# Two layer norms and the products behind them, worked by pairs of token blocks in half-width items

## The chip, the cores and the metric

The kernel runs on one core of a Trainium2 chip. A core has TensorE (matmuls and transposes, results in the eight PSUM banks), VectorE, ScalarE and GpSimd (called DVE, ACT and POOL in the profile), and SyncE (SP), which only starts transfers here. They run their own instruction streams and wait for each other by semaphores. The metric is the time of one execution on the device, in microseconds (us), lower is better.

## The reference

The input is `x`, one sequence of 512 tokens by 1024 features in float32. The first block computes a conditioning vector from `c`, a hybrid mixer (a state-space scan and a forgetting attention), and a feed-forward; the second block a banded attention with a short convolution and a pooling, and another feed-forward. Cut to what matters here:

```
# first block
x = layer_norm(ALPHA * x + (1 + g1) * y, ln1_g, ln1_b)        # y: the mixer's output product
h = x * (1 + sc2) + sh2
ff = square(relu(h @ w_ff_in)) @ w_ff_out                     # 1024 -> 4096 -> 1024
x = layer_norm(ALPHA * x + (1 + g2) * ff, ln2_g, ln2_b)
# second block
h = rms_norm(x, norm1_g)
p = h @ w_in                                                  # q, k, v first: 3 x 512 columns
```

with `layer_norm(x) = (x - mean) / sqrt(var + eps) * g + b` over the 1024 features of a token.

## The kernel before

**Tiles.** The 512 tokens are four blocks `t` of 128. The 1024 features are eight tiles `k` of 128. `x1[:, t]` holds block `t`, tokens on the partitions. A product needs its activations turned, features on the partitions: `a_hi[0][:, k]` and `a_lo[0][:, k]`, each 128 x 512 tokens. Each product is done as three matmuls (`three`, lines 1700 to 1704), high by high, high by low and low by high, because a value is held as a rounded part and a rest.

**Weights.** They come in units of 128 x 2048 through two slots, unit `u` in slot `u % 2`. A unit is loaded into `raw` (SyncE), rounded into `w_hi` (ScalarE, `hi`, line 740, once `ticks` says that the slot's unit before has been used), and its rest `w_lo` is made by four subtractions of 512 columns (GpSimd, `lo`, line 546). TensorE waits for `w_lo_made`, which counts whole units. A unit feeds 48 matmuls of 512 columns. In the feed-forward a unit of `w_ff_in` (`columns`) gives two output tiles of 128 hidden features by 512 tokens, with the weights stationary; in `row_pair` two units give an output of four token blocks by 512 columns, with the activations stationary and weights moving.

**Order.** Every engine's order is written out by hand. At the first norm: VectorE reads the last product's banks, adds (line 1580), and takes statistics per block (`half_stats`, lines 1208 to 1212); GpSimd makes the root (`ln_root`, line 539); VectorE makes the shift (line 1217); ScalarE normalises blocks 0 to 2 whole (`normalize`, line 753), VectorE block 3 (`normalize_last`, line 1225). TensorE turns the blocks (`turn_blocks`, line 1777), 32 transposes, into banks 0 to 7, one bank per feature tile with all four blocks. Then ScalarE makes the high part of each tile (line 748) and its negated rest (line 761), 512 columns each, and VectorE the low part (`split_affine`, line 1161). Between block 2 and the tiles ScalarE rounds the second unit. VectorE then applies gain and bias to `x1` (`gain`, lines 1232 and 1233). The first two output tiles follow the feature tiles as they come (`two_tiles`), the other products behind them.

The second norm, at the end of the first feed-forward, is made in the same way (sum on line 1599) and feeds `row_pair(U_QKV2, ...)`, whose two units give the first 512 of the columns. Then ScalarE sums squares for the RMS norm (`squares`, line 779), reads the product's banks (`read_rows`, line 773), and GpSimd makes the head roots (line 525).

In the feed-forward ScalarE reads a finished tile (line 838), squares it (line 840), and rounds the next but one unit behind the first two tiles of a pair; VectorE makes the hidden tile's low part (lines 1249 and 1149).

## Time and profile before

| | |
|---|---|
| median of 3 runs | 1438.65 us (1436.66 to 1438.85) |
| profiled execution | 1433.96 us, its span 1432.2 us |
| mean granted TensorE clock in it | 0.994 |
| TensorE matmul busy | 1370.6 us, 96% |
| VectorE, ScalarE, GpSimd busy | 698.0, 547.4, 688.3 us |

The span runs from the first to the last instruction of the profiled execution; 1.8 us of its time lie around it. Ends of matmuls are modelled: neighbours overlap in the list, so the distance from start to start is what one costs. The granted clock is a share of full speed.

### The profile page before, as it was taken

Reading aid. Unit: us, or ns where it says so; the run is one execution under the profiler, and the core shown is the slowest. Engines: PE = TensorE matmul, PEld = TensorE weight load, DVE = VectorE, ACT = ScalarE, POOL = GpSimd, SP = SyncE. Lnnn points to the kernel's source line nnn. Section 1 sums busy time; section 2 is a strip of 40 time slices with the busy share of each in tenths; the row PEclk is TensorE's granted clock in tenths of the full one; section 3 lists DMA queues with packets and bytes.
Section 4 is the critical chain, followed back from the end, with each engine's and each line's share of the span. In section 5 each row is a group of like instructions: output and inputs, shape, how many; then the busy total and the mean of one; then the engine's idle time right before and its main releaser. Section 6 shows DMA issues by size and latency. Waiting matters only on the chain.

```text
span 1432.2 us, 17281 instructions
## 1 busy us (share of the span) xinstructions
PE 1370.6 (96%) x6567; PEld 1124.0 (78%) x6567; DVE 698.0 (49%) x1005; ACT 547.4 (38%) x793; POOL 688.3 (48%) x544
## 2 busy tenths in 40 slices
PE   2999999999999999999999998999999999999999
PEld 2887787778777878888888886886788888888887
DVE  6676978788843672141324456357623213132231
ACT  0635454476662262141332316324525223132231
POOL 0453855332346655445445544753644445445442
PEclk9999999999999999999999999999999999999999
DMA  9353445755323432322232232342122332232232
GB/s 331 116 136 93 98 129 173 207 142 150 104 59 130 146 92 88 109 96 88 88 117 88 88 110 72 105 120 77 45 93 89 105 101 88 92 102 99 88 98 78
DMA packets 132249, 158.58 MB, mean 111 GB/s; under 512 B 9469, under 2 KB 93713, under 8 KB 131937
## 3 DMA queue, kind: packets, MB, share of 16 engines
q1 hardware_dynamic: 123760, 146.95, 32.6%
q10 hardware_dynamic: 6240, 5.40, 1.7%
q0 software_dynamic: 2192, 5.49, 1.2%
q8 instruction: 34, 0.56, 0.2%
q14 instruction: 23, 0.18, 0.0%
HBM read 153.47 MB, written 2.26 MB: 109 GB/s over the span
## 4 chain that ended last, share of the span: by engine, by line
PE 81%; DVE 9%; POOL 3%; issue 2%; ACT 2%; DMA 1%; SPq 0%; ACTq 0%; DVEq 0%; POOLq 0%
PE bank L1702 25%; PE bank L1703 24%; PE bank L1704 24%; DVE tmp L1268 3%; POOL w_lo L546 3%; PE bank L1839 1%; DMA arena<-in_w_ada_dram 1%; DVE rinv L1175 1%; PE bank L1970 1%; PE bank L2208 1%; PE bank L1824 1%; ACT w_hi L740 1%; PE bank L1849 1%; PE bank L2026 1%; PE bank L1852 1%
## 5 line engine op out<-in xcount | busy, mean ns | idle before, releaser
L546 POOL TENSOR_TENSOR w_lo<-raw,w_hi 128x512 fp32r<-128x512 f32 x428 | 585.2, 1399 | 605.9 <-ACT w_hi L740 604.7
L1702 PE MATMUL bank<-w_hi,a_hi 128*128 128x512 f32 x928 | 365.3, 394 | 13.3 <-POOL w_lo L546 6.5
L1703 PE MATMUL bank<-w_lo,a_hi 128*128 128x512 f32 x928 | 362.6, 391 | 0.0
L1704 PE MATMUL bank<-w_hi,a_lo 128*128 128x512 f32 x928 | 362.6, 391 | 0.0
L740 ACT ACTIVATE w_hi<-raw 128x2048 fp32r<-128x2048 f32 x107 | 204.7, 1913 | 356.8 <-PE bank L1704 353.6
L1702 PE MATMUL bank<-a_hi,w_hi 128*128 128x512 f32 x800 | 315.7, 395 | 3.4 <-DVE a_lo L1161 2.5
L1703 PE MATMUL bank<-a_lo,w_hi 128*128 128x512 f32 x800 | 312.2, 390 | 0.0
L1704 PE MATMUL bank<-a_hi,w_lo 128*128 128x512 f32 x800 | 312.0, 390 | 0.0
L1702 PEld LDWEIGHTS bank<-w_hi,a_hi 128*128 128x128 f32 x928 | 175.1, 189 | 51.7 <-DVE a_lo L1161 6.2
L1704 PEld LDWEIGHTS bank<-w_hi,a_lo 128*128 128x128 f32 x928 | 175.0, 189 | 36.9
L1703 PEld LDWEIGHTS bank<-w_lo,a_hi 128*128 128x128 f32 x928 | 175.1, 189 | 35.7
L1702 PEld LDWEIGHTS bank<-a_hi,w_hi 128*128 128x128 f32 x800 | 150.7, 188 | 35.4 <-issue 2.7
L1704 PEld LDWEIGHTS bank<-a_hi,w_lo 128*128 128x128 f32 x800 | 150.7, 188 | 31.9
L1703 PEld LDWEIGHTS bank<-a_lo,w_hi 128*128 128x128 f32 x800 | 150.9, 189 | 30.6 <-issue 0.2
L1249 DVE TENSOR_TENSOR tmp<-arena 128x512 f32<-128x512 f32 x64 | 64.6, 1009 | 189.3 <-ACT arena L838 189.3
L838 ACT ACTIVATE arena<-bank 128x512 f32<-128x512 f32 x64 | 38.4, 599 | 210.9 <-PE bank L1704 203.3
L1691 DVE SCALAR_TENSOR_TENSOR arena<-bank,st,arena 128x512 f32<-128x512 f32 x32 | 24.0, 751 | 144.6 <-PE bank L1704 144.6
L1268 DVE SCALAR_TENSOR_TENSOR tmp<-arena,cact,tmp 128x256 f32<-128x256 f32 (+1 forms) x140 | 88.2, 630 | 4.9 <-DMA arena<-in_w_ada_dram 0.3
L1149 DVE TENSOR_TENSOR a_lo<-tmp,a_hi 128x512 fp32r<-128x512 f32 x64 | 66.7, 1043 | 7.2
L1591 DVE TENSOR_TENSOR arena<-bank,arena 128x512 f32<-128x512 f32 x24 | 16.6, 692 | 109.6 <-PE bank L1704 109.6
L787 ACT ACTIVATE arena<-bank,mxs 128x128 f32<-128x128 f32 (+1 forms) x96 | 49.5, 533 | 35.7 <-DVE mxs L1179 35.5
L825 ACT ACTIVATE arena<-bank 128x512 f32<-128x512 f32 (+1 forms) x72 | 33.2, 526 | 22.2 <-PE bank L1839 17.5
(248 smaller groups left out, 1258.6 us busy)
## 6 DMA issues: line engine op xcount, KB each, us to landing
raw<-in_w_mlp_dram SPq DMA_DIRECT2D x32, 1024.0 KB, 5.3
raw<-in_w_in_dram SPq DMA_DIRECT2D x24, 1024.0 KB, 5.2
arena<-in_w_ada_dram SPq DMA_DIRECT2D x18, 1024.0 KB, 6.5
raw<-in_w_ff_in_dram SPq DMA_DIRECT2D x16, 1024.0 KB, 5.4
raw<-in_w_ff_out_dram SPq DMA_DIRECT2D x16, 1024.0 KB, 5.1
raw<-in_w_out_dram SPq DMA_DIRECT2D x12, 1024.0 KB, 5.6
raw<-in_w_in_dram SPq DMA_DIRECT2D x16, 512.0 KB, 5.7
arena<-in_w_ada_dram SPq DMA_DIRECT2D x3, 2048.0 KB, 18.1
```

The source lines that it names most:

```text
L546: last = pool.tensor_tensor(w_lo[:, u0 % 2, cols], raw[:, u0 % 2, cols], w_hi[:, u0 % 2, cols].bitcast(F32), ALU.subtract)
L740: act.activation(w_hi[:, u0 % 2], raw[:, u0 % 2], ACT.Copy).then_inc(w_hi_made, 1)
L787: act.activation(dst[:, QO[q]:QO[q] + n], src(q), ACT.Exp, bias=mxs[:, h % 2, q:q + 1], accum_out=rsum[:, h % 2, q:q + 1]).then_inc(p_made, 1)
L825: act.activation(dst[:, 512 * m:512 * m + n * P], bank[b][:, 0:n * P], ACT.Copy).then_inc(pt_made, 1)
L838: act.activation(rl[:, k % 2], bank[4 * b + j][:], ACT.Relu).then_inc(evac[b], 1)
L1149: dve.tensor_tensor(a_lo[buf][:, k], tmp[:, m0 % 2], a_hi[buf][:, k].bitcast(F32), ALU.subtract)\
L1249: dve.tensor_tensor(tmp[:, k % 2], rl[:, k % 2], rl[:, k % 2], ALU.mult).then_inc(tile_made, 1)
L1268: ins = dve.scalar_tensor_tensor(acc, src(k), cact[:, k:k + 1], acc, ALU.mult, ALU.add)
L1691: dve.scalar_tensor_tensor(x1[:, t, part], bank[4 * b + t][:], st[:, 12 + t:13 + t], x1[:, t, part], ALU.mult, ALU.add).then_inc(evac[b], 1)
L1702: pe.matmul(out_, hi_a, hi_b, start=start, stop=False)
L1703: pe.matmul(out_, hi_a, lo_b, start=False, stop=False)
L1704: return pe.matmul(out_, lo_a, hi_b, start=False, stop=stop)
```

## The change

- An item is a pair of token blocks (256 columns) of one feature tile. `LN_ITEMS` lists 16: features 0 to 3 of blocks 0 and 1, of blocks 2 and 3, then features 4 to 7 in the same order. Transposes go to halves of banks 4 to 7.
- ScalarE normalises blocks 0 and 1, VectorE blocks 2 and 3 in halves, and the statistics of block 3's second half, the four half normalisations and the low parts of the items are interleaved in `last_tokens`. The shift of block 0 comes one block earlier.
- TensorE starts with the first eight transposes and puts the other 24 behind items 1, 3 and 7.
- At the first norm the first four output tiles (`first_columns`) are made in passes: features 0 to 3 with the first unit, then with the second, then features 4 to 7 with the first and the second, in matmuls of 256 columns, 192 in place of 96. The first quarter of the feed-forward is taken out of TensorE's loop.
- At the second norm `first_rows` goes item by item, for two token blocks each, in matmuls of 512 columns.
- The second unit at either norm is rounded on GpSimd in quarters, each followed by its subtraction (`both_parts`), with a semaphore `lo_part` for the first three.
- ScalarE rounds the third unit at the second norm ahead of items 12 to 15, the fourth ahead of the first reads, and the sixth between two pairs of reads. GpSimd makes the row loads ahead of the quarters and the mask behind them.

```diff
+LN_ITEMS = [(pair, 4 * half + k) for half in range(2) for pair in range(2) for k in range(4)]
...
+        def turned_item(pair, k):
+            return bank[4 + 2 * pair + k % 2][:, 256 * (k % 4 // 2):256 * (k % 4 // 2) + 256]
...
+            def both_parts(u0):
+                pool.wait_ge(landed[u0 % 2], 16 * (u0 // 2 + u0 % 2 + pairs_loaded(u0)))
+                pool.wait_ge(ticks, 2 * u0 - 2)
+                for part in range(4):
+                    cols = slice(512 * part, 512 * part + 512)
+                    ins = pool.tensor_copy(w_hi[:, u0 % 2, cols], raw[:, u0 % 2, cols])
+                    if part == 0:
+                        ins.then_inc(w_hi_made, 1)
+                        pool.wait_ge(w_hi_made, u0 + 1)
+                    else:
+                        link(ins)
+                    ins = pool.tensor_tensor(w_lo[:, u0 % 2, cols], raw[:, u0 % 2, cols], w_hi[:, u0 % 2, cols].bitcast(F32), ALU.subtract)
+                    ins.then_inc(lo_part if part < 3 else w_lo_made, 1)
...
-            ln_root(0)
-            pool.wait_ge(xhat_last, 2)
-            lo(U_FF1 + 1)
+            lo(U_WO2 + 4, turn=0)
+            for t in range(1, TB):
+                ln_root(0, t)
+            both_parts(U_FF1 + 1)
...
+            def affine_items(r0, t0, scale, bias, js):
+                def rest(j):
+                    pair, k = LN_ITEMS[j]
+                    act.wait_ge(a_hi_made, t0 + j + 1)
+                    act.wait_ge(a_lo_made, t0 + max(j - 3, 0))
+                    act.activation(rest_item(j), a_hi[0][:, k, tokens(pair)].bitcast(F32), ACT.Identity, scale=-1.0, bias=bias(k)).then_inc(tile_made, 1)
+                for j in js:
+                    pair, k = LN_ITEMS[j]
+                    act.wait_ge(turned, r0 + j // 4 * 4 + 3 + j % 2)
+                    if j % 4 >= 2:
+                        act.wait_ge(a_lo_made, t0 + j - 1)
+                    act.activation(a_hi[0][:, k, tokens(pair)], turned_item(pair, k), ACT.Identity, scale=scale(k), bias=bias(k)).then_inc(a_hi_made, 1)
+                    rest(j)
...
-            for t in range(TB - 1):
+            for t in range(2):
                 normalize(1, t)
-            hi(U_QKV2 + 1)
-            turned_affine(R_N2, T_N2, 0, ...)
+            for js in (range(12), range(12, 16)):
+                affine_items(R_N2, T_N2, ..., js)
+                if js[0] == 0:
+                    act.wait_ge(w_hi_made, U_QKV2 + 2)
+                    hi(U_QKV2 + 2)
-            hi(U_QKV2 + 2)
             squares(2, x1, junk, ln_made, lambda t: 4 + t + 1)
+            hi(U_QKV2 + 3)
...
+            def last_tokens(turn, m0, scale):
+                split_item(0, m0, scale)
+                half_stats(TB - 1, 1)
+                split_item(1, m0, scale)
+                normalize_half(turn, 2, 0)
+                normalize_half(turn, 3, 0)
+                split_item(2, m0, scale)
+                split_item(3, m0, scale)
+                normalize_half(turn, 2, 1)
+                normalize_half(turn, 3, 1)
+                for j in range(4, 16):
+                    split_item(j, m0, scale)
...
+            def first_columns():
+                first_turned(0, N_FF1)
+                for half in range(2):
+                    for n0 in (0, 2):
+                        u = U_FF1 + n0 // 2
+                        if half == 0 and n0 == 0:
+                            pe.wait_ge(w_lo_made, u + 1)
+                        for j in range(8 * half, 8 * half + 8):
+                            pair, k = LN_ITEMS[j]
+                            if n0 == 0:
+                                pe.wait_ge(a_lo_made, T_X1 + j + 1)
+                            elif pair == 0 and k % 2 == 0:
+                                wait_part(u, 0, k // 2)
+                            for n in (n0, n0 + 1):
+                                w = slice(256 * k + P * (n % 2), 256 * k + P * (n % 2) + P)
+                                last = three(bank[n][:, tokens(pair)], w_hi[:, u % 2, w], w_lo[:, u % 2, w],
+                                             a_hi[0][:, k, tokens(pair)], a_lo[0][:, k, tokens(pair)], j == 0, j == 15)
+                                if j == 15:
+                                    last.then_inc(ticks, 1)
+                            if n0 == 0:
+                                turn_behind(0, T_X1, N_FF1, j)
+
+            def first_rows():
+                first_turned(1, N_QKV2)
+                for j, (pair, k) in enumerate(LN_ITEMS):
+                    u = U_QKV2 + k // 4
...
+                    pe.wait_ge(a_lo_made, T_N2 + j + 1)
+                    for t in (2 * pair, 2 * pair + 1):
+                        a, w = slice(P * t, P * t + P), slice(512 * (k % 4), 512 * (k % 4) + 512)
+                        last = three(bank[t][:], a_hi[0][:, k, a], a_lo[0][:, k, a], w_hi[:, u % 2, w], w_lo[:, u % 2, w],
+                                     k == 0, k == KT - 1)
...
+                    turn_behind(1, T_N2, N_QKV2, j)
```

## Rows read from the trace of the kernel before

**Rows 1.** The page, busy time of TensorE: us, share of the span, instructions.
```profile
PE 1370.6 (96%) x6567; PEld 1124.0 (78%) x6567; DVE 698.0 (49%) x1005; ACT 547.4 (38%) x793; POOL 688.3 (48%) x544
```

**Rows 2.** Timeline of TensorE, first norm: start, us, operation, idle before, releaser.
```profile
499.83 0.39 PE L1704 MATMUL bank<-w_hi,a_lo 128*128 128x512 f32 x1
...
505.00 1.11 PE L1777 MATMUL bank<-ident,arena 128*128 128x128 f32 x8 [0.60 <-DVE arena L1225]
508.36 0.47 PE L1702 MATMUL bank<-a_hi,w_hi 128*128 128x512 f32 x1 [2.24 <-DVE a_lo L1161]
...
532.35 0.39 PE L1702 MATMUL bank<-a_hi,w_hi 128*128 128x512 f32 x1
```

**Rows 3.** Timeline of TensorE, second norm.
```profile
858.52 0.39 PE L1704 MATMUL bank<-w_hi,a_lo 128*128 128x512 f32 x1
...
870.75 0.80 PE L1702 MATMUL bank<-w_hi,a_hi 128*128 128x512 f32 x1 [5.99 <-DVE a_lo L1161]
...
894.56 0.39 PE L1702 MATMUL bank<-w_hi,a_hi 128*128 128x512 f32 x1
```

**Rows 4.** Stretches, TensorE: from, to, us, busy, granted clock, DMA share, GB/s.
```profile
510.00:511.00 1.00, 1.00 (x4) 0.50 0.00 0
```

**Rows 5.** Timeline of TensorE, two other waits for weights.
```profile
248.32 0.50 PE L1702 MATMUL bank<-w_hi,a_hi 128*128 128x512 f32 x1 [2.30 <-POOL w_lo L546]
...
454.84 0.61 PE L1702 MATMUL bank<-w_hi,a_hi 128*128 128x512 f32 x1 [1.85 <-POOL w_lo L546]
```

**Rows 6.** Timelines of VectorE and ScalarE, first norm: sums and normalisations.
```profile
496.37 1.09 DVE L1580 TENSOR_TENSOR arena<-arena 128x512 f32<-128x512 f32 x1
...
501.90 0.68 DVE L1580 TENSOR_TENSOR arena<-arena 128x512 f32<-128x512 f32 x1
...
499.38 2.37 ACT L753 ACTIVATE arena<-arena,st 128x1024 f32<-128x1024 f32 x2 [8.03 <-DVE st L1217]
```

**Rows 7.** Groups of ScalarE by line and shape: busy us, mean ns, idle before.
```profile
L748 ACT ACTIVATE a_hi<-bank,mod 128x512 fp32r<-128x512 f32 x24 | 18.5, 780 | 0.7 <-PE bank L1777 0.6
L761 ACT ACTIVATE tmp<-a_hi,mod 128x512 f32<-128x512 f32 x24 | 17.1, 728 | 0.0
...
L825 ACT ACTIVATE arena<-bank 128x512 f32<-128x512 f32 x48 | 26.2, 595 | 19.0 <-PE bank L1839 14.4 <-DMA inv_d<-rinv 4.3
...
L825 ACT ACTIVATE arena<-bank 128x256 f32<-128x256 f32 x24 | 9.3, 389 | 3.2 <-PE bank L1839 3.1
```

**Rows 8.** Timeline of TensorE, score matmuls of 256 columns, and the next.
```profile
368.92 0.33 PE L2026 MATMUL bank<-k_split,q_split 128*128 128x256 f32 x1
369.10 0.28 PE L2027 MATMUL bank<-k_split,q_split 128*128 128x256 f32 x1
369.21 0.34 PE L2026 MATMUL bank<-k_split,q_split 128*128 128x384 f32 x1
```

**Rows 9.** Timelines of ScalarE and GpSimd: the feed-forward's third unit.
```profile
520.39 0.60 ACT L838 ACTIVATE arena<-bank 128x512 f32<-128x512 f32 x1 [4.67 <-PE bank L1704]
...
522.92 1.90 ACT L740 ACTIVATE w_hi<-raw 128x2048 fp32r<-128x2048 f32 x1
...
524.90 6.90 POOL L546 TENSOR_TENSOR w_lo<-raw,w_hi 128x512 fp32r<-128x512 f32 x4 [9.21 <-ACT w_hi L740]
```

**Rows 10.** Groups of GpSimd by line and shape: casts of 512 elements.
```profile
L579 POOL CAST q_split<-ones 64x512 fp32r<-64x512 f32 x4 | 5.0, 1258 | 0.4 <-POOL w_lo L546 0.2
...
L554 POOL CAST arena<-arena 16x512 fp32r<-16x512 f32 x1 | 0.6, 607 | 0.1
```

**Rows 11.** Behind the second norm: timeline of VectorE, ScalarE's group of squares, GpSimd's timeline.
```profile
878.51 1.23 DVE L1232 TENSOR_TENSOR arena<-arena 128x1024 f32<-128x1024 f32 x1 [3.31 <-DMA arena<-in_ln_b_dram]
...
L779 ACT ACTIVATE arena<-arena 128x1024 f32<-128x1024 f32 x12 | 12.7, 1060 | 0.3
...
898.61 5.42 POOL L546 TENSOR_TENSOR w_lo<-raw,w_hi 128x512 fp32r<-128x512 f32 x4 [4.39 <-ACT w_hi L740]
```

**Rows 12.** Timeline of TensorE, first product of the stage behind the second norm's.
```profile
940.22 0.47 PE L1702 MATMUL bank<-a_hi,w_hi 128*128 128x512 f32 x1 [0.88 <-POOL w_lo L546]
```

179 lines of the change are left out of this document (105 added, 74 removed).

## The prediction

> **What bounds the kernel now.** I read the profile page's busy times first [rows 1]: TensorE is busy for 96% of the span, so a change counts only where TensorE waits, runs at the lower clock, or gets more instructions. Then I read its timeline where the diff acts. At the first norm the last output product starts at 499.83, the last transposes run at 505.00, the first product behind them waits another 2.24 and starts at 508.36, and the third weight unit starts at 532.35 [rows 2]. At the second the same steps stand 358.69 later, but the first product waits 5.99 for the fourth low tile and starts at 870.75; the third unit starts at 894.56 [rows 3]. Two units are 96 matmuls, at 0.2267 each (between starts of neighbours at full clock) 21.8 us. They took 24.0 and 23.8: the difference of 2 us is mostly clock, granted at 0.50 (the 1.2 GHz level) behind the first wait [rows 4]; the 0.80 of the matmul at 870.75 shows the same behind the second. Shorter waits can do it too: 1.85 us ahead of 454.84 was followed by matmuls of 0.61, while 2.30 ahead of 248.32 was not (0.50) [rows 5]. From 532.35 to 858.52 are 326.17, and the 1439 matmuls started between need 326.2: TensorE has no slack there, and a wait put there adds itself whole.
>
> So about 8.5 us lie between last product and first product at the first norm, 12.2 at the second. Not all is to be had: 32 transposes stay. Eight take 1.11 with their drain [rows 2], that is 0.12 each, 3.9 for 32.
>
> **First norm: an earlier start.** VectorE's shift of block 0 moves right behind the sum of block 1, which ends at 497.46 [rows 6], and the root on GpSimd moves ahead of the last quarter of the unit before. ScalarE's two normalisations (1.2 each) can then end near 500.75 instead of 501.75 [rows 6]; statistics and root of block 1 stand between them. Eight transposes later ScalarE starts on item 0 at about 501.45. An item is two activations of 256 columns. At 512 columns they take 0.78 and 0.73; going from 512 to 256 columns took 0.21 off a copy from PSUM (0.595 to 0.389) [rows 7]. So 0.57 and 0.52; the second waits for the end of the first, with hand-overs 1.12 a pair. VectorE is free at 502.6, when the sum of block 3 ends [rows 6], and needs 0.5 for its part: first product at 503.2, 5.2 earlier than now. But 16 items of 1.12 are 17.9 on ScalarE, against 8 pairs of at most 1.51 now, and item 7 is ready only at 511.1.
>
> **First norm: the products.** Each item lets TensorE do 6 matmuls of 256 columns. No product of this kernel has that shape; the nearest are score matmuls of 256 columns with the same weight load, of which one started 0.11 after the other [rows 8]. The bounds are 0.11 and, from half of 213 plus the 14 ns that stand over 512 columns' 213, 0.12; if a pair like the one behind 368.92 (0.18 to the next) were the rule, 0.18. I take 0.12: 0.72 per item, less than 1.12, so TensorE follows ScalarE through the first half and ends item 7 at 511.9. Behind it come 8 transposes (1.0), pass 2 of the first half (48 matmuls, 5.8) and pass 1 of the second half (5.8): 524.4, and 0.5 for a low clock while it works in drips, so 524.9. Pass 2 ends it at 530.7. That alone would be 1.7 earlier than 532.35.
>
> The Trainium skill, TensorE: Matmul & The Clock Gate, Back-to-back issue gap, gives N/2.4 + 2.5 ns between matmuls at full clock, 109 ns for 256 columns and 216 for 512. The rows have 227 for 512, so I stay with the rows; by the page's figure the 96 matmuls ahead of 524.9 that nothing hides would take 1.0 less, and the sum below would be 1.9 instead of 2.9.
>
> **First norm: what is late next.** Now the first unit is given back after its own 48 matmuls, at about 521.4, and the second is used for 10.9 more. In the new order both units stay in use to the last half pass: the first unit's slot is free at 524.9, and only 5.8 of work are left. The way to the third unit's weights is in the rows [rows 9]: ScalarE starts its reads at 520.39, two reads and two squares (2.53) stand ahead of the rounding at 522.92, which takes 1.90, and GpSimd's four subtractions take 6.90, to 531.80; today that is 0.55 ahead of need. The same chain from 524.9 is 2.5 + 1.9 + 0.1 + 6.9 + 0.1: 536.4. VectorE's gain pass now ends near 530 and its hidden tiles follow, so the subtractions run beside it as they do now; with less beside them they take 5.4 [rows 11]. TensorE stands still for 5.7. The wait is as long as that of [rows 3], so I add its clock loss, 1.9. First norm: 536.4 - 532.35 + 1.9 = 6.0 **lost**; bounds 2 (subtractions at 5.4, clock kept throughout) and 8.5 (the low clock all through the first half too).
>
> **The quarters on GpSimd.** A quarter copy of 128x512 is not in the trace. Nearest are casts of 0.6 and 1.26 for 512 elements [rows 10]; with a subtraction of 1.3 to 1.7 a quarter takes 2 to 3. Block 3's statistics and root end at 504.8; from there part 0 is ready by 507.9 and part 3 by 517; needed from 512.9 on. At the second norm all is 358.7 later behind two row loads, and the need comes at 876.6. Both stay hidden behind the first half, and would cost only if two quarters took over 8. Taking the rounding (1.90) off ScalarE is what lets item 0 follow the transposes at once; that gain is in the starts above.
>
> **Second norm.** Here weights are the moving side: matmuls stay at 512 columns and their number stays. First product at 503.2 + 358.7 = 861.9; an item now carries 6 x 0.2267 = 1.36 us of work, more than ScalarE's 1.12, so TensorE is the pace. 21.8 of matmuls, 24 transposes among them (3.0), 0.1 of waits, 0.7 for the clock: second unit ends at 887.5, 7.1 earlier than 894.56. The third unit is ready: its slot is free behind item 7 (861.9 + 8 x 1.36 + 2.0 of transposes + 0.8: 875.7), ScalarE rounds it behind item 11, GpSimd ends by 884.6. The fourth is not. ScalarE does items 12 to 15 only after that rounding: 875.7 + 2.0 + 4.5 + 0.6 = 882.8 for the last low tile. Then VectorE's gain pass, 8 operations of 1.23 [rows 11] and a little for its start beside the subtractions, to 892.9; the last square with its sum 1.25, the fourth unit's rounding 1.9, behind the squares in ScalarE's queue, subtractions 5.4 [rows 11]: ready at 901.7. Needed at 887.5 + 10.9 = 898.4. A wait of 3.3, and 1.5 for the clock, between nothing [rows 5] and the 2.0 of [rows 3]. Today the fourth starts at 894.56 + 10.9 = 905.4. So 3.7 gained at its start, 2.2 once the clock is paid.
>
> Further on, today TensorE waits 0.88 at 940.22 for the weights of the next stage, behind two head roots on GpSimd [rows 12]. The sixth unit's rounding moves ahead of the second pair of reads (1.3), which starts that row of GpSimd work 1.3 sooner, so 0.9 goes. Second norm: 2.2 + 0.9 = 3.1 **gained**; bounds 1 (a full clock loss at both places) and 6 (none).
>
> Other moved steps (row loads, ahead of the quarters; the mask, behind them) issue as many DMAs as before and are wanted 10 us later. The unrolled first quarter adds no work.
>
> **Sum.** 6.0 - 3.1 = 2.9 lost. The profiled execution took 1433.96 (span 1432.2 and 1.8 around it); with the change 1436.9. The median of the runs is 4.7 above it, so 1438.65 + 2.9 = 1441.6, just over the 0.2% (2.9 us) that a measurement of this kernel can tell from no change.
>
> **Rivals.**
> - *Clock kept* (ends on the other side): no low clock behind the new waits, as ahead of 248.32 [rows 5]. Takes off 1.9 + 1.5 + 0.5 + 0.7 = 4.6: 1437.0, no change. Any saving over 0.1 decides. Against it: the wait of 5.7. Chance 0.13.
> - *Subtractions undisturbed*: 5.4 instead of 6.9 for the third unit takes off 1.5: 1440.1, no change. Against it, [rows 9]. 0.19.
> - *Third unit in time*: TensorE reaches it at 530.7 and goes on. 1.7 + 3.1 gained: 1433.8, faster. It decides, with the clock then kept, if the chain behind 524.9 takes under 7.6, where I count 11.5; for it speaks only that the chain's rounding and reads might overlap. 0.12.
> - *Half-size matmuls at 0.18*: 96 x 0.06 = 5.8 more: 1447.4, slower. Speaks for it one pair of starts. 0.09.
> - My forecast: 0.47, of which 0.07 falls within 0.2%.
>
> Slower 0.40 + 0.09 = 0.49, within 0.2% 0.13 + 0.19 + 0.07 = 0.39, faster 0.12. The range leaves out the third and fourth rival: 1436 to 1446.5, with the forecast's own case from 1439.5 to 1444.
>
> **What would show it.** Right: first products 5 us earlier at the first norm, 9 at the second; starts of 256-column matmuls 0.12 apart; one wait of 4 to 6 us for GpSimd's low part ahead of the third unit of the feed-forward, matmuls of 0.63 behind it; a wait of about 3 ahead of the fourth unit at the second norm. Wrong: no wait ahead of the third unit, or subtractions well under 6.9 there, or the gain pass starting before the last low tile.

## The result, and the profile after

The changed kernel takes 1448.74 us (median of 4 runs, 1448.13 to 1448.97), the kernel before in the same session 1437.66 (4 runs): ratio 1.0078, 95% interval 1.0061 to 1.0095. Timed again with the experiments it was 1.0070 (1.0043 to 1.0096). It is slower; 1441.6 was predicted.

The page's line of busy times, after:

```profile
PE 1382.3 (96%) x6663; PEld 1138.1 (79%) x6663; DVE 704.2 (49%) x1023; ACT 552.1 (38%) x821; POOL 694.2 (48%) x552
```

TensorE has its 96 matmuls more and is as full as before [rows 1]; the span grew from 1432.2 to 1446.9. The timeline of TensorE around the first norm:

```profile
504.39 0.39 PE L1773 MATMUL bank<-w_hi,a_lo 128*128 128x512 f32 x1
...
508.50 0.55 PE L1771 MATMUL bank<-a_hi,w_hi 128*128 128x256 f32 x1 [1.83 <-DVE a_lo L1218]
...
535.71 0.28 PE L1772 MATMUL bank<-a_lo,w_hi 128*128 128x256 f32 x1
535.83 0.28 PE L1773 MATMUL bank<-a_hi,w_lo 128*128 128x256 f32 x1
541.40 0.77 PE L1771 MATMUL bank<-a_hi,w_hi 128*128 128x512 f32 x1 [5.28 <-POOL w_lo L576]
...
545.38 0.48 PE L1771 MATMUL bank<-a_hi,w_hi 128*128 128x512 f32 x1
```

Counted from the start of the last product before the norm, the first product comes after 4.11 us (8.53 before [rows 2]), the half passes end 31.6 us after it, and then TensorE waits 5.28 for the third unit, which starts after 37.01, not 32.52 as before. Nine matmuls at the half clock (granted 0.50; 0.427 apart) follow. The timelines of ScalarE and GpSimd say what it waited for:

```profile
532.44 1.90 ACT L771 ACTIVATE w_hi<-raw 128x2048 fp32r<-128x2048 f32 x1
...
534.42 6.83 POOL L576 TENSOR_TENSOR w_lo<-raw,w_hi 128x512 fp32r<-128x512 f32 x4 [11.01 <-ACT w_hi L771]
```

It is the chain of [rows 9], whose subtractions now begin 30.0 us after the last product and not 25.1. The timeline of TensorE behind the second norm:

```profile
869.65 0.39 PE L1773 MATMUL bank<-w_hi,a_lo 128*128 128x512 f32 x1
...
873.70 0.76 PE L1771 MATMUL bank<-w_hi,a_hi 128*128 128x512 f32 x1 [1.79 <-DVE a_lo L1218]
...
915.12 0.79 PE L1771 MATMUL bank<-w_hi,a_hi 128*128 128x512 f32 x1 [4.41 <-POOL w_lo L576]
...
920.83 0.49 PE L1772 MATMUL bank<-w_lo,a_hi 128*128 128x512 f32 x1
...
953.20 0.47 PE L1771 MATMUL bank<-a_hi,w_hi 128*128 128x512 f32 x1 [1.48 <-POOL w_lo L576]
```

The first product comes 4.05 us after the last one instead of 12.23 [rows 3], but the fourth unit is waited for 4.41 and started after 45.47; thirteen matmuls at the half clock follow, and the wait for U_CP (the seventh unit, the first of the next stage) grew from 0.88 [rows 12] to 1.48. The first product of that stage stands 83.55 us after the last one before the norm, 1.85 later than before (81.70). What the fourth unit and U_CP's wait for, in the timelines of VectorE, ScalarE and GpSimd:

```profile
894.11 0.48 DVE L1218 SCALAR_TENSOR_TENSOR a_lo<-bank,mod,tmp 128x256 fp32r<-128x256 f32 x1 [0.51 <-ACT tmp L806]
894.51 1.79 DVE L1301 TENSOR_TENSOR arena<-arena 128x1024 f32<-128x1024 f32 x1
...
904.84 1.06 ACT L826 ACTIVATE arena<-arena 128x1024 f32<-128x1024 f32 x1 [1.24 <-DVE arena L1302]
...
906.02 1.92 ACT L771 ACTIVATE w_hi<-raw 128x2048 fp32r<-128x2048 f32 x1
...
908.02 11.98 POOL L576 TENSOR_TENSOR w_lo<-raw,w_hi 128x512 fp32r<-128x512 f32 x8 [0.62 <-ACT w_hi L771]
...
931.16 7.14 POOL L576 TENSOR_TENSOR w_lo<-raw,w_hi 128x512 fp32r<-128x512 f32 x4 [5.33 <-ACT w_hi L771]
938.38 2.15 POOL L538 TENSOR_SCALAR st<-head_rs 128x32 f32<-128x32 f32 x1
```

Last low tile, gain pass, four squares, rounding, subtractions: one chain. The fourth unit's subtractions end as TensorE starts, at 915.1, so they took 7.1 us (the row of eight is two units).

**Where 14.7 us of span went.** By the last products before the norms, the spans differ by 4.56 ahead of the first, 6.57 from the first to the second (365.26 against 358.69), and 3.57 from there to the end. The first of the three lies in code that the change doesn't touch. The stretches of TensorE (from, to, us, busy, granted clock, DMA share, GB/s) show it; these are the kernel before in its first profile, then in a second one, then the changed kernel:

```profile
180.00:200.00 20.00, 18.82 (x97) 1.00 0.29 96
240.00:260.00 20.00, 17.70 (x84) 1.00 0.86 252
1035.00:1060.00 25.00, 22.84 (x110) 1.00 0.28 90
```
```profile
180.00:200.00 20.00, 18.82 (x81) 0.83 0.31 104
240.00:260.00 20.00, 17.70 (x78) 0.91 0.88 260
1035.00:1060.00 25.00, 22.84 (x123) 1.00 0.24 73
```
```profile
180.00:200.00 20.00, 18.82 (x82) 0.83 0.31 99
240.00:260.00 20.00, 17.70 (x78) 0.91 0.89 257
1035.00:1060.00 25.00, 22.84 (x129) 0.93 0.30 96
```

The kernel before loses the same clock in some executions: against its second profile (span 1436.9, last products at 504.06 and 862.97) the change costs 10.0. Of the 3.57 behind the second norm, 1.7 is clock at 1035 to 1060 (0.07 of 25 us), far from the change; the kernel before has full clock there in both profiles.

### The profile page after: what moved, and what is told of

It reads as the page before. It is cut to its first block, busy times and chain, and to the rows that moved or that the text cites. A ratio compares the mean times of both kernels' runs of the same rounds, so it can differ in the third digit from the quotient of the medians.

```text
span 1446.9 us, 17550 instructions
## 1 busy us (share of the span) xinstructions
PE 1382.3 (96%) x6663; PEld 1138.1 (79%) x6663; DVE 704.2 (49%) x1023; ACT 552.1 (38%) x821; POOL 694.2 (48%) x552
## 4 chain that ended last, share of the span: by engine, by line
PE 78%; DVE 10%; POOL 5%; issue 3%; ACT 2%; DMA 1%; SPq 0%; ACTq 0%; POOLq 0%; DVEq 0%
PE bank L1771 24%; PE bank L1773 23%; PE bank L1772 23%; POOL w_lo L576 4%; DVE tmp L1337 3%; PE bank L1968 1%; DMA arena<-in_w_ada_dram 1%; ACT w_hi L771 1%; PE bank L2099 1%; PE bank L2337 1%; PE bank L1953 1%; DVE rinv L1232 1%; PE bank L1978 1%; PE bank L2155 1%; PE bank L1981 1%
## 5 line engine op out<-in xcount | busy, mean ns | idle before, releaser
L576 POOL TENSOR_TENSOR w_lo<-raw,w_hi 128x512 fp32r<-128x512 f32 x420 | 574.6, 1399 | 602.5 <-ACT w_hi L771 602.5
L1771 PE MATMUL bank<-w_hi,a_hi 128*128 128x512 f32 x928 | 367.9, 396 | 13.5 <-POOL w_lo L576 10.9
L771 ACT ACTIVATE w_hi<-raw 128x2048 fp32r<-128x2048 f32 x105 | 200.9, 1913 | 346.9 <-PE bank L1773 342.8
L1771 PE MATMUL bank<-a_hi,w_hi 128*128 128x512 f32 (+1 forms) x832 | 323.1, 388 | 8.6 <-POOL w_lo L576 6.8
L1772 PE MATMUL bank<-a_lo,w_hi 128*128 128x512 f32 (+1 forms) x832 | 319.0, 383 | 0.0
L1773 PE MATMUL bank<-a_hi,w_lo 128*128 128x512 f32 (+1 forms) x832 | 318.9, 383 | 0.0
L1771 PEld LDWEIGHTS bank<-a_hi,w_hi 128*128 128x128 f32 x832 | 157.9, 190 | 39.7 <-issue 9.4
L1773 PEld LDWEIGHTS bank<-a_hi,w_lo 128*128 128x128 f32 x832 | 157.8, 190 | 30.5
L1772 PEld LDWEIGHTS bank<-a_lo,w_hi 128*128 128x128 f32 x832 | 158.1, 190 | 29.7 <-issue 0.2
L1250 DVE TENSOR_TENSOR arena<-bank,arena 64x256 f32<-64x256 f32 x48 | 29.5, 614 | 25.2 <-PE bank L1981 24.6
```

Of the source, the lines that this page charges most:

```text
L576: last = pool.tensor_tensor(w_lo[:, u0 % 2, cols], raw[:, u0 % 2, cols], w_hi[:, u0 % 2, cols].bitcast(F32), ALU.subtract)
L771: act.activation(w_hi[:, u0 % 2], raw[:, u0 % 2], ACT.Copy).then_inc(w_hi_made, 1)
L1250: last = dve.tensor_tensor(by_query(att_pair(h)[own(h % 2)], side), value_out(side), inverse_rows(h, side), ALU.mult)
L1771: pe.matmul(out_, hi_a, hi_b, start=start, stop=False)
L1772: pe.matmul(out_, hi_a, lo_b, start=False, stop=False)
L1773: return pe.matmul(out_, lo_a, hi_b, start=False, stop=stop)
```

## The experiments

Two stages are compared for each kernel, both from TensorE's timeline: A, from the last product before the first norm to the last before the second; B, from there to the end of the span. Both leave out the early clock, but not the half clock inside them. So how well a stage repeats was read from kernels that have the same code in it. Stage A with the first norm of before was profiled six times: 357.59 to 359.32. With the changed one it took 364.65 to 365.65 (three), with the changed one by quarters 358.61 to 359.66 (three). Stage B with the second norm of before took 573.68 and 573.93, with the changed one as it is 572.69 to 577.26 (seven). A difference of 1 to 2 us between two single profiles therefore tells little. B is split at U_CP's first product as well: from there to the end are 491.95 to 492.05 us in eight profiles and 493.46 to 493.70 in the other eight, whatever the waits ahead; the two groups differ in how long the half clock was granted there.

Medians and ratios are of whole times, which hold the early clock too. The kernel before had medians of 1437.64, 1434.34, 1437.90 and 1436.90 in the four sessions of the experiments; its times lie in two groups, so the recorded ratio need not be the quotient of the medians (third by quarters: 0.9999, while the medians give 1.0023).

| kernel | last products | A | B | of B, up to U_CP | median us | ratio, 95% |
|---|---|---|---|---|---|---|
| before | 499.83, 858.52 | 358.69 | 573.68 | 81.70 | | |
| before again | 504.06, 862.97 | 358.91 | 573.93 | 81.94 | | |
| changed | 504.39, 869.65 | 365.26 | 577.25 | 83.55 | 1448.74 | 1.0078 (1.0061 to 1.0095) |
| changed again | 503.99, 869.64 | 365.65 | 577.26 | 83.62 | 1446.02 | 1.0070 (1.0043 to 1.0096) |
| fourth early | 500.05, 864.70 | 364.65 | 571.00 | 77.47 | 1437.99 | 1.0018 (0.9999 to 1.0036) |
| third by quarters | 505.64, 864.25 | 358.61 | 572.85 | 80.81 | 1437.61 | 0.9999 (0.998 to 1.0018) |
| rounding first | 499.21, 864.04 | 364.83 | 574.46 | 82.41 | 1440.18 | 1.0047 (1.0027 to 1.0066) |
| first unit whole | 504.34, 866.69 | 362.35 | 573.01 | 81.02 | 1440.26 | 1.003 (1.0013 to 1.0048) |
| kept busy | 499.49, 863.55 | 364.06 | 574.45 | 82.50 | 1440.61 | 1.0043 (1.0026 to 1.0061) |
| rounded on ScalarE | 500.96, 868.28 | 367.32 | 578.22 | 84.74 | 1451.67 | 1.0099 (1.0062 to 1.0137) |
| second norm as it is, alone | 499.28, 858.21 | 358.93 | 572.69 | 80.71 | 1437.87 | 1.0011 (0.9989 to 1.0032) |
| second norm alone, fourth early | 510.77, 869.66 | 358.89 | 569.64 | 76.02 | 1434.45 | 0.9983 (0.9967 to 1.0) |
| both repairs | 498.61, 857.89 | 359.28 | 569.71 | 76.02 | 1433.63 | 0.9978 (0.9959 to 0.9996) |
| both, roots later | 504.21, 863.87 | 359.66 | 567.13 | 73.65 | 1429.76 | 0.9943 (0.9922 to 0.9964) |
| second alone, fourth early, roots later | 503.62, 861.21 | 357.59 | 568.69 | 75.23 | 1431.78 | 0.9956 (0.9937 to 0.9975) |
| before, root later | 504.51, 863.83 | 359.32 | 573.57 | 81.55 | 1434.46 | 0.9984 (0.9969 to 0.9999) |

**The kernel before, once more.** No edit.

> The kernel before, unchanged, profiled once more. In the two profiles at hand everything before the first norm stands 4.56 us later after the change (last product's start 504.39 against 499.83), in code that the change does not touch, and the stretch behind U_CP's first product is 1.7 us longer. If that is the variation of single executions (the profiled one of before was among its fast ones, 1433.96 us against a median of 1437.66), this profile stands at a span of some 1435 to 1437 us with its last product before the first norm at 501 to 504. If the changed program itself costs that time, this profile repeats 499.8 and 1432.2.

It took 1438.67 us, with the clock rows shown above. The early difference is a matter of execution, not of the change. These two profiles agree to 0.2 us in A and 0.3 in B; over all runs a stage repeats less well, as said above.

**The fourth unit's rounding after the first square.**

```diff
 # ScalarE
-            squares(2, x1, junk, ln_made, lambda t: 4 + t + 1)
+            squares(2, x1, junk, ln_made, lambda t: 4 + t + 1, (0,))
             hi(U_QKV2 + 3)
+            squares(2, x1, junk, ln_made, lambda t: 4 + t + 1, (1, 2, 3))
 # GpSimd
-            rms_root(2, EPS2)
             lo(U_QKV2 + 3)
+            rms_root(2, EPS2)
```

> The changed kernel with the fourth unit behind the second norm rounded after the first of the four squares on ScalarE, not after the fourth, and its subtraction on GpSimd ahead of the root. Theory (the fourth unit is late because its rounding stands behind the gain pass and the squares): the rounding starts near 899.6 us instead of 906.0, the subtraction ends near 909 instead of 915.1, the wait of 4.41 us and the clock loss of 2.85 us behind it go, 7 us in all: about 1441.5 us. Rival (the wait is set by GpSimd and by contention with VectorE, not by the order): the subtraction, now beside the gain pass, takes 9 us or more, and less than 3 us are gained: 1446 us or more.

Timelines of ScalarE, GpSimd and TensorE:

```profile
892.70 1.06 ACT L826 ACTIVATE arena<-arena 128x1024 f32<-128x1024 f32 x1 [3.52 <-DVE arena L1303]
...
895.04 1.92 ACT L771 ACTIVATE w_hi<-raw 128x2048 fp32r<-128x2048 f32 x1 [1.20 <-PE bank L1774]
...
897.04 7.29 POOL L576 TENSOR_TENSOR w_lo<-raw,w_hi 128x512 fp32r<-128x512 f32 x4 [6.72 <-ACT w_hi L771]
...
929.23 0.50 PE L1772 MATMUL bank<-w_hi,a_hi 128*128 128x512 f32 x1 [1.67 <-POOL w_lo L576]
```

The wait for the fourth unit and the half clock behind it are gone, and B is 6.25 shorter, 2.7 under before. The order was the cause of the wait: beside the gain pass the subtractions took 7.29, hardly more than 7.1, so the rival falls. What the wait cost is read up to U_CP, from runs with the late fourth unit and the same clock behind the first product: 77.47 against 82.41 and 82.50 (rounding first, kept busy), and 76.02 against 80.71 for the second norm alone, below. That is 4.7 to 5.0 us. Of B's 6.25, 1.1 is a half clock that lasted longer in the changed kernel's own profiles; and the runs with the fourth unit early give 1.5 to 1.6 back to the clock behind U_CP, so that in B 3.1 to 3.5 are left. The whole time, 1437.99, lies below the 1441.5 expected, but it holds the early clock, which this profile (last product at 500.05) did not lose and the changed kernel's did. The next late unit shows up, the sixth, with 1.67.

**The first unit over all items, then the second in whole tiles.**

```diff
-                for half in range(2):
-                    for n0 in (0, 2):
...
+                for j in range(16):            # first unit, 256 columns
...
+                    turn_behind(0, T_X1, N_FF1, j)
+                for n in range(2):             # second unit, 512 columns
+                    column_tile(U_FF1 + 1, n, 0, bank[2 + n][:])
 # ScalarE, ahead of the feed-forward
+            act.wait_ge(w_lo_made, U_FF1 + 2)
```

> The changed kernel with the first unit behind the first norm multiplied over all sixteen items in 256 columns, and the second unit after it in whole tiles of 512 columns, so that the first slot is free after the sixteenth item. Theory (the third unit is late because both first units are held to the last half pass): the first unit ends near 525 us, the second near 535.5, the third unit is rounded by 529 and ready by 536, its wait falls from 5.28 us to under 1, and the 2.1 us of clock behind it go: 6 to 7 us gained, about 1442 us. Rival (matmuls of half the width are the cost): 48 of the 96 extra matmuls go, at most 48 x 0.013 = 0.6 us more than their columns ask for; if this were the cause, the wait would stay and the time fall to 1448 us. Second rival: TensorE, which has the work of one unit alone while the items are made (0.72 us for each 1.0), stays at the half clock to the sixteenth item, and 3 us of the gain go back: 1445 us.

Timelines of ScalarE, GpSimd, VectorE and TensorE:

```profile
528.04 1.91 ACT L771 ACTIVATE w_hi<-raw 128x2048 fp32r<-128x2048 f32 x1
...
530.03 8.63 POOL L576 TENSOR_TENSOR w_lo<-raw,w_hi 128x512 fp32r<-128x512 f32 x4 [6.66 <-ACT w_hi L771]
...
529.63 1.22 DVE L1302 TENSOR_TENSOR arena<-arena 128x1024 f32<-128x1024 f32 x1
530.88 2.20 DVE L1303 TENSOR_TENSOR arena<-arena 128x1024 f32<-128x1024 f32 x1
533.00 2.31 DVE L1302 TENSOR_TENSOR arena<-arena 128x1024 f32<-128x1024 f32 x1
...
538.81 0.77 PE L1772 MATMUL bank<-a_hi,w_hi 128*128 128x512 f32 x1 [1.94 <-POOL w_lo L576]
```

The rounding came 4.35 us earlier against the last product (23.70 after it, 28.05 in the changed kernel), as the theory has it. But the subtractions, now beside VectorE's gain pass, took 8.63 instead of 6.83, and slowed that pass too: its operations take 1.22 ahead of them and 2.20 to 2.31 beside them. 1.94 of wait stayed, with a half clock behind it. A is 2.9 shorter, under half of the 6 to 7 expected. The span is 7.2 shorter, but 4.2 of that lies in B, where code and waits (4.4 and 1.5) are those of the changed kernel.

**TensorE kept busy through the wait.**

```diff
                         first_columns()
+                        for m in range(22):
+                            pe.matmul(bank[4][:], a_hi[0][:, m % 8, 0:P], a_hi[0][:, m % 8], start=True, stop=True)
```

> The changed kernel with 22 matmuls of 512 columns added behind the half passes, into a bank that the next tile starts anew, so that TensorE works through most of the wait of 5.28 us for the third unit. Theory (the half clock after that wait is a cost of its own, 2.1 us): the third unit starts no earlier than now, near 541.4 us, but the nine matmuls at the half clock behind it run at the full one: 1446.6 us. Rival (the half clock costs nothing there because GpSimd's next units are late as well): the time stays at 1448.7 us.

TensorE's timeline:

```profile
532.14 5.18 PE L2232 MATMUL bank<-a_hi 128*128 128x512 f32 x22
537.27 0.47 PE L1771 MATMUL bank<-a_hi,w_hi 128*128 128x512 f32 x1
```

The third unit starts 37.78 after the last product, no earlier than in the changed kernel, and what follows runs at full clock: from its start to the second norm's last product 326.28, as before (326.17), against 328.25. So 2.0 of A is the half clock alone; 0.8 of it was given back ahead of the start. The whole time fell to 1440.61, not to the 1446.6 expected: the profile also lacks the early half clock (last product at 499.49), and its B is 2.8 shorter with the same code and waits, so the whole time doesn't measure this edit.

**The third unit handed over by quarters.**

```diff
 # TensorE, first tile of the third unit
+                        for k in range(KT):
+                            if k % 2 == 0 and k < 6:
+                                pe.wait_ge(lo_part, 3 + k // 2 + 1)
+                            elif k == 6:
+                                pe.wait_ge(w_lo_made, u0 + 3)
+                            last = column_step(u0 + 2, 0, 0, bank[4][:], k)
 # GpSimd: each of the four subtractions signals
+                    ins.then_inc(lo_part if part < 3 else w_lo_made, 1)
```

> The changed kernel with the third unit behind the first norm handed over by quarters: GpSimd signals each of its four subtractions, and TensorE's first tile of that unit waits for a quarter at a time (the loop over the quarters of the feed-forward is written out for its first turn on GpSimd and TensorE). Theory (the wait of 5.28 us is the time that the whole unit's rounding and subtraction take, and only the first quarter of it has to be waited for): the first product of the third unit starts near 32 us after the last product before the norm, not 37.0, right behind the half passes; the four quarters end at the same time as before, so its first tile, 5.5 us long, ends near 38.5 instead of 44.7 (with the half clock): 5 to 6 us gained in this stage. Rival: TensorE stutters through the first tile (1.7 us a quarter of which it works 1.4) and the clock falls all the same: 3.5 us gained.

Timelines of GpSimd and TensorE:

```profile
534.99 6.93 POOL L574 TENSOR_TENSOR w_lo<-raw,w_hi 128x512 fp32r<-128x512 f32 x4 [10.37 <-ACT w_hi L783]
...
536.95 0.47 PE L1783 MATMUL bank<-a_hi,w_hi 128*128 128x512 f32 x1 [0.26 <-POOL w_lo L574]
...
538.56 0.50 PE L1783 MATMUL bank<-a_hi,w_hi 128*128 128x512 f32 x1
```

The subtractions are as late and as long as before, but the third unit's first product comes 31.31 after the last product, not 37.01, and each quarter arrives just as the last is used up (0.16 to 0.22 lost at the start of each). The clock stays at full through all of A, which is 358.61: 6.65 shorter and equal to before. The same code gave 359.28 and 359.66 in the two variants with both repairs, where the half clock stands behind the first product as in the changed kernel, so the quarters give back 5.0 to 7.0, 6.0 on the means. Nearly all of the first norm's loss was this wait and its clock; over three profiles against six, 0.5 is left of it, within the spread, and no gain shows.

**The third unit's rounding ahead of the reads.**

```diff
 # ScalarE, first turn of the feed-forward written out
-                        if j == 2:
+                        if early and b == 0:
+                            if j == 0:
+                                hi(u0 + 2)
+                        elif j == 2:
                             hi(u0 + 2 * b + 2, i, 8)
```

> The changed kernel with ScalarE rounding the third unit ahead of the first two reads and squares of the hidden tiles instead of behind them (its loop written out for the first turn). Theory: the rounding starts at 30.1 instead of 32.4 us of 'after' counted, 2.3 us earlier, and the subtraction and the third unit with it: the wait of 5.28 us falls to some 3.0, the half clock behind it stays: 2.3 us gained in this stage. Rival: the subtraction, now beside the gain pass on VectorE, lengthens from 6.8 to 8.6 us, as it did where the first unit was finished early, and only 0.5 us are gained.

Timelines of ScalarE, GpSimd and TensorE:

```profile
525.47 1.92 ACT L771 ACTIVATE w_hi<-raw 128x2048 fp32r<-128x2048 f32 x1 [6.06 <-PE bank L1777]
...
527.47 7.49 POOL L576 TENSOR_TENSOR w_lo<-raw,w_hi 128x512 fp32r<-128x512 f32 x4 [9.23 <-ACT w_hi L771]
...
535.10 0.77 PE L1775 MATMUL bank<-a_hi,w_hi 128*128 128x512 f32 x1 [3.97 <-POOL w_lo L576]
```

The rounding is 1.8 earlier, the subtractions 0.7 longer, the third unit 1.1 earlier (2.3 expected), A 0.4 to 0.8 shorter than in the changed kernel's two profiles. The rival is nearer: who moves these subtractions forward moves them into VectorE's gain pass.

**The changed kernel, timed again.**

> The changed kernel itself, timed again. Six profiles so far fall into two groups by the granted clock of 180 to 200 and 240 to 260 us, code that no variant touches: 1.00 in both (before, and the variants with the fourth unit early and with TensorE kept busy) or 0.83 and 0.91 (before again, the changed kernel, the variant with the first unit whole), 4.6 us apart by the last product before the first norm. The kernel before shows both: 12 of its 29 times lie from 1432.0 to 1435.4, 17 from 1437.5 to 1441.5. Theory (the four times of the changed kernel, 1448.13 to 1448.97, all had the half clock there, and the change itself costs 10 us): some of its times now lie near 1444, and the median between 1444 and 1449. Rival (the changed program always loses that clock): all lie from 1448 to 1449.

Its times were 1442.96 to 1443.52 (three, mean granted clock 0.990) and 1448.52 to 1451.59 (three, 0.985 to 0.987): the theory holds, its first four times were all of the longer sort. This profile (1448.63) is again of the longer sort and repeats stage B to 0.01 us; an execution of the shorter sort was never profiled.

**Second norm alone, fourth unit early.** First norm's code as before; second norm's as changed, with the edit above.

> The first norm as in the kernel before, the second norm by pairs of blocks as in the changed one, with the fourth unit rounded after the first square. Theory (the first norm's part is worth -5.9 to -6.6 us, the second norm's with this order +2.8): from the last product before the second norm to the end 571.0 us, as in the variant with the fourth unit early, against 573.7 and 573.9 in the two profiles of before; from the first norm's last product to the second's 358.8 as before; 2.8 us faster than before, about 1434.8 us. Rival (the new second norm pays only because the stage before it was disturbed): within 1 us of before.

A is as before, B 569.64, 4.0 to 4.3 under it, more than the 2.8 expected. The whole time, 0.9983 (0.9967 to 1.0000), shows less of it than the stages do, which leave the early clock out. This kernel's profile lost more of it than any other (last product at 510.77), and its 12 times lie from 1429.23 to 1441.07; the early stretches of TensorE:

```profile
240.00:260.00 20.00, 17.70 (x70) 0.83 0.89 258
280.00:300.00 20.00, 17.80 (x95) 0.83 0.57 159
```

**Both repairs.** The two edits above together.

> The changed kernel with both repairs: the third unit behind the first norm handed over by quarters, and the fourth unit behind the second norm rounded after the first square. Theory (the two late units are the whole of the loss): from the first norm's last product to the second's 358.6 us, as with the quarters alone, and from there to the end 571.0 us, as with the fourth unit early alone: 2.7 to 3 us less than before in the same stages (358.7 + 573.7), a time about 0.2% under before. Rival (the clock gives back what the waits lose: the two gains do not add): equal to before within 1 us.

The gains add: A 359.28, B 569.71, and the time is 0.22% under before.

**Both repairs, and the head roots one unit later.**

```diff
             lo(U_QKV2 + 4)
-            head_root(0)
             lo(U_QKV2 + 5)
+            head_root(0)
+            lo(U_CP)
             head_root(1)
```

> Both repairs, and on GpSimd the two roots of the head norms (5.4 us each) moved one unit back, behind the subtractions of the sixth unit and of U_CP. Theory: the waits for those two units, 1.67 and 0.88 us with the fourth unit early, go, and 2.5 us are gained over the variant with both repairs, 4.2 if the half clock near 979 us (of 'start of the profile' counted) goes with them. Rival (the root that is now late holds VectorE's normalisation and TensorE's transposes of q and k): the gain is under 1 us.

TensorE's waits from 860 to 1000 us (releaser: us in total, times, longest):

```profile
PE bank L2362 <- ACT arena L847: 2.9, 1, 2.9
PE bank L1785 <- DVE a_lo L1232: 1.8, 1, 1.8
...
```

TensorE waits for no weight unit any more, and no wait of its own goes back to the later roots; B is 2.6 shorter than with both repairs (567.13 against 569.71), 2.4 of it up to U_CP. This is the best version: 0.57% under before (0.36% to 0.78%).

> First norm as in the kernel before; second norm by pairs with the fourth unit rounded after the first square; and the two roots of the head norms behind the subtractions of the sixth unit and of U_CP. Theory: 569.6 us from the second norm's last product to the end with the second norm alone; 2.5 us less with the two waits gone: 567 us, 6.5 us less than before. Rival (roots late): 569.6 stays.

The same roots without the first norm's change give 0.9956: B is 568.69, only 0.95 under the variant without the later roots, where 2.5 was expected. The same waits are gone; but a half clock stands behind the first product here (0.83 in the 10 us from the last product, 1.00 in the variant without the later roots). Against the variant that has it too (fourth early), the later roots give 2.24 up to U_CP (75.23 and 77.47), and 2.37 without it on either side (73.65 and 76.02). Both intervals of the whole time overlap widely; whether the first norm's halves are worth keeping was not told apart.

**The second units rounded on ScalarE.**

```diff
 # ScalarE, at both norms
             for t in range(2):
                 normalize(0, t)
+            hi(U_FF1 + 1)
             affine_items(...)
 # GpSimd: quarters of subtractions only
-                    ins = pool.tensor_copy(w_hi[:, u0 % 2, cols], raw[:, u0 % 2, cols])
```

> The changed kernel with the second unit behind each norm rounded by ScalarE in one instruction of 1.9 us, between the normalisations and the first item, as the kernel before did; GpSimd only subtracts, by quarters. Theory (the quarters on GpSimd are hidden and keep ScalarE free): the first items are made 1.9 us later at either norm, the stage behind the first norm takes 367 us instead of 365.3, and the one behind the second 579 instead of 577.3: 3.8 us slower than the changed kernel. Rival (GpSimd's rounding beside VectorE slows the first items and pays nothing): no slower than the changed kernel.

The first products come 5.10 and 5.08 us after the last ones, 1.0 later than in the changed kernel and not the 1.9 expected; the third unit starts at 38.67 instead of 37.01, the fourth at 47.83 instead of 45.47. A is 1.7 to 2.1 longer, B 1.0. So the quarters on GpSimd pay at these starts. The whole time, 1.0099 (1.0062 to 1.0137, four runs), is not told apart from the changed kernel's.

**Second norm as it is, alone; and a root moved in the kernel before.**

> First norm as in the kernel before, second norm exactly as in the changed kernel (fourth unit after the four squares). The stretch from the second norm's last product to the end was 577.25 and 577.26 us in two profiles of the changed kernel, but 572.85 to 574.46 us in three variants whose code from there on is the same and whose waits there are the same (4.4 and 1.5 us). Theory (those waits cost what the pairs gain, and the rest is how much of the half clock falls on work): 572.9 to 574.5 us, within 1 us of before, and a time within 0.2% of before. Rival (the second norm's part by itself costs the 3.4 us that the changed kernel shows): 577 us, and a time 0.25% above before.

B is 572.69, 1.0 to 1.2 under before, at the same waits (4.40 and 1.45) as in the changed kernel; the whole time is that of before (1.0011, 0.9989 to 1.0032). TensorE from the last product to U_CP's, first in this kernel, then in the changed one:

```profile
858.21:938.92 80.71, 72.30 (x331) 0.98 0.26 90
```
```profile
869.65:953.20 83.55, 75.09 (x330) 0.94 0.26 87
```

The same products kept TensorE busy for 72.30 us here and 75.09 there, at 0.98 and 0.94 of the clock: 2.79 of the 2.84 between the two stretches. Three stretches hold the whole difference in B, 4.56. They are the first 10 us, the fourth unit's wait with what follows, and 30 to 36 us behind U_CP's first product, in this kernel and then in the changed one:

```profile
858.21:868.21 10.00, 7.45 (x40) 1.00 0.50 187
898.21:908.21 10.00, 5.93 (x20) 0.83 0.32 105
968.72:974.72 6.00, 3.39 (x22) 1.00 0.19 65
```
```profile
869.65:879.65 10.00, 7.43 (x34) 0.83 0.51 190
911.05:921.05 10.00, 5.93 (x14) 0.66 0.34 107
983.00:989.00 6.00, 3.35 (x11) 0.74 0.23 80
```

TensorE is busy for the same time in each and does less in it. The fourth unit starts 44.07 us after the last product instead of 45.47 (1.40), six matmuls behind it run at the half clock instead of thirteen (1.44), and from U_CP's first product to the end are 491.98 instead of 493.70 (1.72). Third by quarters and first unit whole, with the late fourth unit as well and 1.00 in the first 10 us, start it at 44.09 and 44.12; rounding first and kept busy, with 0.83 there, at 45.64 and 45.65.

The second norm's part as it is gains 0.7 to 1.2 us up to U_CP where the clock stays full behind the first product (80.71 to 81.02 against 81.70 and 81.94, three profiles) and loses 0.5 to 1.9 where it doesn't (82.41 to 83.62, four). The whole time shows neither.

> The kernel before with one of the two roots of the head norms moved behind U_CP's subtraction, and nothing of the change. Theory (the gain of the moved roots in the variants comes from the waits for the sixth unit and U_CP, of which before has only the second, 0.88 us): 0.9 us faster than before, within what the measurement tells. Rival (the half clock that before has near 973 us comes from that wait and goes with it): 2.6 us faster.

Only one of the two roots is moved here. B is 573.57, 0.1 to 0.4 shorter; the wait of 0.88 is replaced by one of 0.5. The half clock near 973 us is gone, and one near 1041 stands in its place (granted 0.89 at 1035 to 1050, 1.00 in the same stretch of before). The ratio is 0.16% under 1 with an interval that ends at 0.9999. Up to U_CP it is 81.55, 0.15 to 0.4 shorter, where both later roots gave 2.2 to 2.4 with the fourth unit early. So most of that gain exists only once the waits ahead of the roots are gone, as far as one moved root can show it.

## Why the prediction was wrong

1441.6 was predicted, with 1446.5 as the upper end; 1448.7 was measured. The sign was right, and so was the first norm. The step that failed is the second norm's sum: 3.1 gained was predicted, 3.3 to 3.6 lost was measured.

- **First norm, earlier start.** 3.4 us after the last product; measured 4.11. ScalarE's items take 0.55 and 0.51 (0.57 and 0.52 predicted).
- **First norm, products.** 0.12 between starts of 256 columns, measured 0.12 (535.71 to 535.83); half passes ended 31.6 after the last product, predicted 30.9. The rival of 0.18 is out.
- **First norm, what is late next.** The step that carried the forecast: third unit ready 36.6 after the last product, wait 5.7, clock 1.9, loss 6.0. Measured 37.0, 5.28, 1.9 (541.40 to 545.38 holds nine matmuls, 3.98 less 9 x 0.2267), loss 6.57 against the first profile of before, 6.35 against the second. The subtractions took 6.83. By quarters nearly all of the loss is gone, by filling the wait the clock's part is gone: mechanism and both terms are shown, and the rivals of a third unit in time, undisturbed subtractions and a clock kept are out.
- **Quarters on GpSimd.** Hidden, as predicted; copies took 0.60 to 0.80, near the lower bound. Rounding on ScalarE instead costs 1.7 to 2.1 and 1.0 in the stages.
- **Second norm: the fourth unit.** Predicted: ready 43.2 after the last product, 3.7 gained at its start, 2.2 after the clock. The chain was right. Its term that was too small in every profile is the subtractions: **5.4 was predicted, 7.1 was measured** beside ScalarE's reads and VectorE's 2048-element pass. The gain pass ended 35.1 after the last product (34.4 predicted), but 33.7 in the second norm alone, whose first products had the full clock. Ready at 45.5, so 1.4 gained.
- **Second norm: its clock.** Behind the wait 1.5 was predicted and 2.8 lost (915.12 to 920.83 holds thirteen matmuls: 5.71 - 2.95), so -1.4 instead of +2.2. The second norm alone, with the same wait, lost 1.4 there (902.28 to 905.00 holds six): the mechanism was right, and its size differs from profile to profile.
- **Second norm: U_CP's wait.** "0.9 goes" was wrong. The sixth unit's rounding was not held by the reads it was moved past but by its slot, which the late fourth unit frees late: its subtractions start 61.5 after the last product, 61.2 before. Behind them one small multiplication, beside VectorE's normalisation of q, took 2.15 us against 0.23. The wait grew to 1.48. With the fourth unit early it is 0.88 again.
- **Second norm: clock that the sum holds at nothing.** 1.7 us more is lost behind U_CP. Against before it lies at 1035 to 1060. Against the second norm alone, which has that loss too (granted 0.93 in the same stretch, there 1020.72 to 1045.72), it lies at 983 to 989.
- **What the miss is made of.** From 3.1 gained to 3.57 lost are 6.7 us: 2.3 the fourth unit's later start, 1.3 the longer half clock behind it, 1.4 the rest up to U_CP, where the wait grew instead of going, 1.7 the clock behind U_CP. With the second norm alone the same code gives 1.0 to 1.2 in B, the lower bound of the prediction's 1 to 6. So 4.5 of the 6.7 come from how the clock fell in the changed kernel's own profiles: 1.4 ahead of the fourth unit, 1.4 behind it, 1.7 behind U_CP. Why it falls so in both of them, and not in the variants with the same waits (B 572.85 to 574.46), is not settled; those variants reach the second norm at another time after the first.
- **The profile as base.** "The median of the runs is 4.7 above it" was taken as spread around a sum. It is a term: half clock at 180 to 260 us in some executions, in code that the change doesn't touch. By their length and mean clock (0.986 to 0.987) all four first times of the changed kernel had it, and that was luck: three of six later ones took 1443.0 to 1443.5 at 0.990. Such a time lies in the prediction's range, but 9 us above the shorter sort of before, not 2.9.

## What to carry to other kernels

Finishing two stages' weights together instead of one after the other moves the release of the first slot; look what stands behind that release before counting an earlier start. A consumer that waits for a whole unit can mostly start on its first quarter: here that gave back about 6 us (5.0 to 7.0), where two attempts to produce the unit earlier gave 0.4 to 0.8 and 2.9 to 3.3. A gain in the whole time that the edited stage doesn't show is not the edit's, and a stage wants more than one profile of the same code. When the span of one profile lies well under the median of the runs, look for the stretches of lower clock that it doesn't have before taking it as a base.

## What was unexpected of the hardware

- TensorE's granted clock differs between executions of one kernel in the same code: 1.00 or 0.83 at 180 to 200 us, 1.00 or 0.91 at 240 to 260, 4.2 us by the first norm (499.83 and 504.06), and up to 10.9 in a variant with the same code there (510.77). The times of before lie in two groups that differ in the mean granted clock as well: 12 of 29 at 1432.0 to 1435.4 (0.993 to 0.995) and 17 at 1437.5 to 1441.5 (0.989 to 0.992).
- The same wait of 4.4 us for the fourth unit went with a mean granted clock of 0.94 in the stage to U_CP in the changed kernel and of 0.98 in the one with the second norm alone, with TensorE's idle times alike in both. The first product behind the second norm came 4.03 to 4.06 us after the last, with the same two idle times (0.76 to 0.78 and 1.78 to 1.79), in twelve profiles: in six the granted clock of the first 10 us was 0.83, in six 1.00.
- GpSimd and VectorE slow each other. Four subtractions of 512 columns on GpSimd took from 5.0 us to the 8.63 shown above, and VectorE's 1.22 us operations beside the latter took up to 2.31: both lengthen together. Bringing one engine's work forward therefore paid less than its time.
- Stalls of 0.16 to 0.26 us at each quarter left the clock at full; single ones of 1.94, 3.97 and 5.28 at the same place had the half clock behind them. One of 1.67 ahead of the sixth unit, with the fourth unit early, had not.
